# GLA chunks on one core: level products that move half the queries, seven level buffers, and the mixers' steps in other slots

## What is computed

```
def step(S, inp):
    qc, kc, vc, gc = inp
    Bc = jnp.cumsum(gc, axis=1)
    o_inter = jnp.einsum('blhd,bhdv->blhv', qc * jnp.exp(Bc), S)
    decay = jnp.exp(jnp.where(causal, Bc[:, :, None] - Bc[:, None, :], -jnp.inf))
    A = jnp.einsum('blhd,bshd,blshd->bhls', qc, kc, decay)
    o_intra = jnp.einsum('bhls,bshv->blhv', A, vc)
    BL = Bc[:, -1]
    S_new = jnp.exp(BL)[..., None] * S + jnp.einsum('bshd,bshv->bhdv', kc * jnp.exp(BL[:, None] - Bc), vc)
    return S_new, o_inter + o_intra
```

## Time and profile before

| | us |
|---|---|
| median of 3 runs | 2832.42 (2826.41 to 2833.7) |
| the profiled execution's own time | 2834.81 |
| its span | 2832.7 |
| PE busy | 2692.1 |
| DVE busy | 1515.3 |
| ACT busy | 1023.8 |
| mean granted clock of TensorE | 0.98 of full speed |

### The profile page before, as it was taken

One profiled execution on the slowest core, in us unless ns is written; L12 is line 12 of the kernel. 1 busy time (PEld: TensorE's weight loads), 2 busy tenths in 40 slices (PEclk: granted clock), 3 DMA queues, 4 the chain that ended last, 5 costly groups with the idle time before them and its releaser, 6 DMA issues.

```text
span 2832.7 us, 38394 instructions
## 1 busy us (share of the span) xinstructions
PE 2692.1 (95%) x16018; PEld 2416.0 (85%) x16018; DVE 1515.3 (53%) x2348; ACT 1023.8 (36%) x1453; POOL 0.2 (0%) x4
## 2 busy tenths in 40 slices
PE   5999999999999999988899999999899999999996
PEld 4889898877988998888889978997676978999996
DVE  4533464655366663466545675346764367544335
ACT  3444344432334333443333343344431334222222
POOL 0000000000000000000000000000000000000000
PEclk9999999999999999999999999999999999999998
DMA  4454435443325223532232333344224333322222
...
DMA packets 181727, 331.48 MB, mean 117 GB/s; under 512 B 19476, under 2 KB 98964, under 8 KB 181556
## 3 DMA queue, kind: packets, MB, share of 16 engines
...
...
## 4 chain that ended last, share of the span: by engine, by line
PE 84%; DVE 9%; ACT 3%; DMA 3%; issue 2%; SPq 0%; DVEq 0%; ACTq 0%
PE ps L775 74%; PE ps L926 2%; DMA w_stage<-w_down_in 1%; PE ps L995 1%; PE ps L989 1%; DVE n_xs L1386 1%; DVE Y L1383 1%; ACT w_hi L1022 1%; DVE w_lo L1307 1%; DMA w_stage<-w_in_in 1%; DVE n_normed L1402 1%; PE ps L853 1%; DVE Y L1351 1%; PE ps L882 1%; DVE HL L1398 1%
## 5 line engine op out<-in xcount | busy, mean ns | idle before, releaser
L775 PE MATMUL ps<-HH,w_lo 128*128 128x288 f32 (+1 forms) x3696 | 1024.4, 332 | 11.5 <-DVE HL L1398 6.7
L775 PE MATMUL ps<-HL,w_hi 128*128 128x288 f32 (+1 forms) x3696 | 1010.5, 328 | 0.0
L775 PE MATMUL ps<-HH,w_hi 128*128 128x288 f32 (+1 forms) x3696 | 1010.3, 328 | 0.0
L775 PEld LDWEIGHTS ps<-HH,w_lo 128*128 128x128 f32 x3696 | 631.4, 189 | 75.5 <-issue 18.8
L1307 DVE TENSOR_TENSOR w_lo<-w_stage,w_hi 128x1024 fp32r<-128x1024 f32 x396 | 483.9, 1222 | 364.2 <-ACT w_hi L1022 363.3
L775 PEld LDWEIGHTS ps<-HL,w_hi 128*128 128x128 f32 x3696 | 630.1, 189 | 49.4
L775 PEld LDWEIGHTS ps<-HH,w_hi 128*128 128x128 f32 x3696 | 630.4, 189 | 47.2
L1022 ACT ACTIVATE w_hi<-w_stage 128x1024 fp32r<-128x1024 f32 x396 | 416.2, 1053 | 412.4 <-PE ps L775 277.7
L775 PE MATMUL ps<-hid_hi,w_lo 128*128 128x288 f32 (+1 forms) x1056 | 302.4, 341 | 73.1 <-DVE Y L1351 54.9
L1351 DVE TENSOR_TENSOR Y<-ps,Y 128x512 f32<-128x512 f32 (+1 forms) x320 | 227.2, 722 | 159.2 <-PE ps L775 157.8
L775 PE MATMUL ps<-hid_lo,w_hi 128*128 128x288 f32 (+1 forms) x1056 | 294.9, 334 | 0.0
...
## 6 DMA issues: line engine op xcount, KB each, us to landing
...
```

The source lines that it names most:

```text
L775: mm = pe.matmul(ps[:, grp.bank + t, 0:W], wsl(w, k), x[:, k, t * W:(t + 1) * W], start=(q == 0 and m == 0), stop=(q == len(ks) - 1 and m ...
```

## The change

It has these parts.

1. A level's product moves only the queries of the second blocks: 64 columns instead of 128 (`q` in `level`), with the same 128 keys as weights. Four level results of 64 columns then share a PSUM bank in pairs (`LEVEL_BANK`), the masks have 64 columns for a level, and a merge writes only the second halves of A. The last level (w = 1) takes the keys as they are, so it has one argument and one factor instead of two.
2. There are seven level buffers. `vt` and `y_gated` share a place, as do `y_normed` and `k_decayed`; `vt` is loaded by a step of its own (`lvt`).
3. `lx` becomes `la1` (arguments of the decayed keys and of levels 0 to 2), `la2` (arguments of levels 3 to 6, `k_decayed`, `q_decayed`) and `la3` (factors of levels 0 to 3); `l1` makes the factors of levels 4 to 6 ahead of its merges. With u at G8, G10, G12, G14 (block 0's mixer) and G6 to G14 (block 1's), `la1` stands at the G unit u - 2, `la2` at the U unit u - 1, `la3` and `la` at the G unit u, `l1` and `l2` at the two D units, `lb` at U, `le` at G, and `lvt` at U.
4. W of the GLA layer comes five units later in block 0's case, behind U15 instead of G14, and two units later in block 1's, behind the second D instead of G16. The norm behind the first of them takes its eight `post` steps in pairs, and its `rstd` now hangs on a G unit with two D units behind it.
5. The mLSTM's steps of block 1 are put at other units: a chunk's `me` and the next one's `ma` stand together at a U unit each time. Those of block 0 stay where they were.

```
-        self.puts(B0[22:41])
+        self.puts(B0[22:46])
         self.wout(1, 0)
-        self.puts(B0[41:-2] + A1[:1] + B0[-2:] + A1[1:16])
+        self.puts(B0[46:-2] + A1[:1] + B0[-2:] + A1[1:16])
         self.proj(1, 1, 0, NPROJ)
-        self.puts(A1[16:47])
+        self.puts(A1[16:49])
         self.wout(1, 1)
-        self.puts(A1[47:-2] + B1[:1] + A1[-2:] + B1[1:])
+        self.puts(A1[49:-2] + B1[:1] + A1[-2:] + B1[1:])
...
-    u = mix(plan, 0, 0, at["P", 0, 0, 20, 0], 4)
+    u = mlstm(plan, 0, [(u, u + 1, u + 3, u + 4) for u in range(at["P", 0, 0, 22, 0], at["P", 0, 1, 13, 0], 4)])
...
-    u = mix(plan, 0, 1, at["G", 0, 0, 0, 0], 5)
+    u = at["G", 0, 0, 0, 0]
+    u = mlstm(plan, 1, [(u + 1, u + 3, u + 4, u + 7)] + [(v, v + 2, v + 5, v + 6) for v in range(u + 7, u + 25, 6)])
...
-    u = mix(plan, 1, 0, at["P", 1, 0, 18, 0], 6)
+    u = gla(plan, 0, at["P", 1, 0, 22, 0], [at["G", 0, 1, i, 0] for i in (8, 10, 12, 14)])
...
-    u = norm(2, 0, u + 1, ones, twos)
+    u = norm(2, 0, u + 1, twos, twos)
...
-    u = mix(plan, 1, 1, at["P", 1, 1, 18, 0], 6)
+    u = gla(plan, 1, at["P", 1, 1, 22, 0], [at["G", 1, 0, i, 0] for i in (6, 8, 10, 12, 14)])
...
+def gla(plan, blk, first, slots):
+    tag = plan.tag
+    tag(first, "lload", CHUNKS[blk][0])
+    for c, u in zip(CHUNKS[blk], slots):
+        tag(u - 2, "la1", c)
+        tag(u - 1, "la2", c)
+        tag(u, "la3", c)
+        tag(u, "la", c)
+        tag(u + 1, "l1" if c < NC else "l2", c)
+        if c < NC:
             tag(u + 2, "l2", c)
             tag(u + 3, "lb", c)
             tag(u + 4, "le", c)
-            if c != chunks[-1] or blk:
-                tag(u + 4, "lx", c + 1)
-            u += pace
-        u += 5 - pace
+            if c + 1 in CHUNKS[blk]:
+                tag(u + 5, "lvt", c + 1)
     if blk:
-        e, a = ("me", "ma") if layer == 0 else ("le", "la")
-        tag(u, a, NC)
-        u += 1
-        if layer:
-            tag(u, "l2", NC)
-            u += 1
-        for half in range(2):
-            for b in range(NB):
-                tag(u + b // 4, "ss", layer, NB * half + b)
-            u += 2
-            tag(u, "sh", layer, half)
-            u += 2
-        tag(u, e, NC)
-        u += 1
-    return u
+        return samples(plan, 1, u + 2, "le")
+    return u + 5
...
+def samples(plan, layer, u, last):
+    tag = plan.tag
+    for half in range(2):
+        for b in range(NB):
+            tag(u + b // 4, "ss", layer, NB * half + b)
+        tag(u + 2, "sh", layer, half)
+        u += 3
+    tag(u, last, NC)
+    return u + 1
...
+    LEVEL_BANK = ((3, 0), (3, 256), (2, 0), (2, 256), (0, 0), (0, 256), (1, 0), (3, 0))
+    def LEVEL(c, v):
+        return NLV * c + v if c < NC else NLV * NC + v - 4
...
-            def level(c, v, n):
-                x = g.x
-                b = (3, 2, 0, 1)[v % 4]
+            def level(c, v):
+                x, n = g.x, SIZE(c)
+                b, at = LEVEL_BANK[v]
                 if v < NLV:
-                    pe.wait_ge(s["level_ready"], (NLV * c if c < NC else NLV * NC - 4) + v + 1)
+                    pe.wait_ge(s["level_ready"], LEVEL(c, v) + 1)
                 for h in range(H):
+                    k = x.XL[:, v, h, 0:n] if v < NLV - 1 else x.QK[:, H + h, 0:n]
                     if v < NLV:
-                        lhs = rhs = x.XL[:, (NLV * c + v if c < NC else NLV * NC + v - 4) % 4, h, 0:n]
+                        w = LEVELS[v]
+                        m = n // 2
+                        q = x.XL[:, v, h, 0:n].rearrange("p (b u t) -> p b u t", u=2, t=w)[:, :, 1, :]
                     else:
-                        lhs, rhs = x.QK[:, H + h, 0:n], x.QK[:, h, 0:n]
-                    mm = pe.matmul(ps[0:n, M0 + b, h * L:h * L + n], lhs, rhs, start=True, stop=True)
+                        m, q = n, x.QK[:, h, 0:n]
+                    mm = pe.matmul(ps[0:n, M0 + b, at + h * m:at + (h + 1) * m], k, q, start=True, stop=True)
                 mm.then_inc(s["level_done"], 1)
             def l1(c):
-                for v in range(4):
-                    if v == 1:
-                        pe.wait_ge(s["k_copied"], NC + 1 + c + 1)
-                    if v == 2:
-                        pe.wait_ge(s["v_copied"], NC + 1 + c + 1)
-                    level(c, v, L)
+                level(c, 0)
+                level(c, 1)
+                pe.wait_ge(s["k_copied"], NC + 1 + c + 1)
+                level(c, 2)
+                level(c, 3)
             def l2(c):
-                if c == NC:
-                    pe.wait_ge(s["k_copied"], NC + 1 + c + 1)
-                    pe.wait_ge(s["v_copied"], NC + 1 + c + 1)
-                for v in range(4, 8):
-                    if c < NC:
-                        pe.wait_ge(s["merged"], 8 * c + v - 3)
-                    level(c, v, SIZE(c))
+                pe.wait_ge(s["v_copied"], NC + 1 + c + 1)
+                pe.wait_ge(s["k_copied"], NC + 1 + c + 1)
+                for v in range(4, NLV):
+                    level(c, v)
+                if c < NC:
+                    pe.wait_ge(s["merged"], 8 * c + 2)
+                level(c, NLV)
...
+                level_args(c, *((0, 3) if c < NC else (4, NLV)))
+            def la2(c):
+                x, n = g.x, SIZE(c)
+                q, k = x.QK[:, 0:H, 0:n], x.QK[:, H:2 * H, 0:n]
+                if c < NC:
+                    level_args(c, 3, NLV)
                 dve.wait_ge(s["qk_landed"], 16 * (NC + 1 + c + 1))
+                dve.wait_ge(s["kd_exp"], c + 1)
+                dve.tensor_tensor(x.KD[:, :, 0:n], x.KD[:, :, 0:n], k, ALU.mult).then_inc(s["kd_ready"], 1)
                 dve.wait_ge(s["eb"], c + 1)
                 dve.tensor_tensor(x.QW[:, :, 0:n], x.QW[:, :, 0:n], q, ALU.mult).then_inc(s["q_ready"], 1)
-                dve.wait_ge(s["kd_exp"], c + 1)
-                dve.tensor_tensor(x.KD[:, :, 0:n], x.KD[:, :, 0:n], k, ALU.mult).then_inc(s["kd_ready"], 1)
-                level_factors(c, v0, v1)
+            def la3(c):
+                level_factors(c, *((0, 4) if c < NC else (4, NLV)))
             def merge(c, v0, v1):
                 x, n = g.x, SIZE(c)
                 A = x.A[0:n, :, 0:n]
                 for v in range(v0, v1):
-                    i = 8 * c + (v if c < NC else v - 4)
-                    dve.wait_ge(s["level_done"], i + 1)
-                    if v == v0:
-                        wait(dve, s["num"], NC + c)
-                    wait(dve, s["merged"], i)
-                    dve.copy_predicated(A, g.lmask[0:n, v, 0:n].unsqueeze(1).to_broadcast([n, H, n]),
-                                        heads((3, 2, 0, 1)[v % 4], n)[0:n]).then_inc(s["merged"], 1)
+                    done = {0: 1, 2: 3, 4: 5}.get(v, v)
+                    i = 8 * c + (0 if c < NC else -4)
+                    dve.wait_ge(s["level_done"], i + done + 1)
+                    if c in (0, 4, NC) and v == v0:
+                        dve.wait_ge(s["cleared"], 1 + c // 4)
+                    wait(dve, s["num"], NC + c)
+                    wait(dve, s["merged"], i + v)
+                    b, at = LEVEL_BANK[v]
+                    if v < NLV:
+                        w, m = LEVELS[v], n // 2
+                        shape = [n, H, m // w, w]
+                        mask = g.lmask[0:n, v * L // 2:v * L // 2 + m].rearrange("p (b t) -> p b t", t=w)
+                        dve.copy_predicated(halves(A, w, 1), mask.unsqueeze(1).to_broadcast(shape),
+                                            ps[0:n, M0 + b, at:at + H * m].rearrange("p (h b t) -> p h b t", h=H, t=w)
+                                            ).then_inc(s["merged"], 1)
+                    else:
+                        mask = g.lmask[0:n, NLV * L // 2:NLV * L // 2 + n]
+                        dve.copy_predicated(A, mask.unsqueeze(1).to_broadcast([n, H, n]),
+                                            ps[0:n, M0 + b, 0:H * n].rearrange("p (h t) -> p h t", h=H)
+                                            ).then_inc(s["merged"], 1)
             def l1(c):
-                level_args(c, 4, 4)
+                level_factors(c, 4, NLV)
                 merge(c, 0, 4)
-                level_args(c, 4, NLV)
-                level_factors(c, 4, NLV)
             def l2(c):
-                if c == NC:
-                    dve.wait_ge(s["num"], 2 * NC)
-                    dve.memset(g.x.A[:, :, :], 0.0).then_inc(s["cleared"], 1)
-                    dve.wait_ge(s["cleared"], 3)
-                if c in (0, 4):
-                    dve.wait_ge(s["cleared"], 1 + c // 4)
-                merge(c, 4, 8)
+                merge(c, 4, NLV + 1)
```

149 lines of the change are left out of this document (75 added, 74 removed).

## The result

The changed kernel takes **2789.73 us** (median of 4 runs, 2785.85 to 2797.36), the kernel before 2832.91 beside it (4 runs, 2826.41 to 2833.7). The ratio is 0.9847, with a 95% interval of 0.9834 to 0.986: 43 us or 1.5% faster. The prediction said 2795 and gave 2768 to 2824. The profiled execution took 2786.02 us, 48.8 less than that of before; its span is 2784.2 us, its mean granted clock 0.987.

The account below looks back on a forecast made before the run. Bound: PE's waits for DVE's down-projection eviction around the mixers, plus slow clock behind them. Savings of 43.4, 12.0, 5.1 and 12.0 us, less new costs, took 2834.8 to 2797.5; median forecast 2795 us, range 2768 to 2824.

Parts of the forecast that it names:

- The level products: Level products of full chunks on PE: weight load of 128 keys sets the spacing, so moving 64 columns saves 0.
- Block 0's waits: D-unit waits in block 0's mixer: 3.6 us per chunk instead of 8.4, 14.4 over four chunks.
- (a): W of layer 1, block 0: U15 in between hides `y_lo`, removing a 3.7 us wait and 1.4 of clock, -5.1.
- (b): W in block 1, now directly behind the sample sequences' `le`: a new wait of about 2.3 us, +2.3.
- (c): Layer 1's sample steps now start at a D unit: shorter waits and no clock fall, -1.6 - 9.4 and -1.0.
- (d): Norm behind block 0's W: `rstd` on a G unit and paired `post` steps make DVE late at D units, +5.
- (e): mLSTM: `me` with `ma` at a U unit waits 1.2 us four times, once before; two 1.1 waits go, +1.4.
- Cheap products: Rival for level products: weight load hides behind the stream, 64 columns cost 0.067 us each; 2776 us, chance 0.12.
- the clock falls at half-wide products: Rival: PE streaming half the time for 3.5 us, twice a chunk, lowers its clock; 2822 us, chance 0.15.
- The waits only move: Rival: DVE meets each D unit among the chunks as late as before; 2842 us, chance 0.08.
- slower: Rival: the `k_decayed` wait keeps the clock low through chunk products, 9.4 us per chunk; 2870 us, chance 0.05.
- No new waits: Rival: ACT's exponentials don't delay `w_hi` and DVE keeps pace, so the chunks' 23.5 us go; 2771 us, chance 0.10.

Follow-up runs that it names:

- second trace: The changed kernel timed once more, unaltered, in a later set of runs beside the kernel before: 2793.69 us, ratio 0.986.
- the two experiments on widths: Half-wide level products and merges alone in the kernel before: ratio 1.001; the changed kernel with only 64 keys as level weights (incomplete output): ratio 0.9804.
- half-query experiment: The kernel before with only the half-wide level products and half-wide merges added: 2836.07 us against 2833.81, ratio 1.001.

## Why the prediction was right, point by point

**The ledger.** The prediction's terms add up to 17.5 us less idle time and 19.8 less busy time, 37.3 in all. Measured were 27.3 and, without the 9.3 us of the dense stretch, 11.9, which is 39.2 (24.4 and 15.3 in the second trace). The medians differ by 43 us, 40.6 in the second set. So the sum came close partly by luck: the idle time fell by 7 to 10 us more than summed, the chunks' new waits above all, the clock gave 4.5 to 8 less, and the two nearly cancel. By places, in us:

| term | predicted | measured |
|---|---|---|
| level products | 0 | 0 (53.0 against 52.6 busy) |
| the six long waits | -43.4 | -43.4, all gone |
| new waits, block 0's chunks | +14.4 | 1.5 + 2.28 + 2.23 + 2.21 = +8.2 |
| new waits, block 1's chunks | +9.1 | 2.43 + 2.37 + 2.37 = +7.2 |
| W of block 0, its wait | -3.7 | -3.7 |
| W of block 1 | +2.3 | +2.2 |
| sample steps and D unit, their waits | -2.6 | 0.65, less 2.63: -2.0 |
| the norm | +5 | 6.4, less the 2.6 it had: +3.8 |
| mLSTM | +1.4 | 7.8, less the 4.9 it had: +2.9 |
| D unit beside the later norm (2.87 for 4.30) | not named | -1.4 |
| idle elsewhere | 0 | -1.1 |
| clock behind six waits, W and samples; new falls | -22.8 + 3 | -11.9 |
| dense stretch of the last feed-forward | 0 | -9.3, not of the change |

**What bounds the kernel** was right: PE's waits at D units among the chunks and what the clock lost behind them. The places, the releaser and the double cost are all in the two traces.

**The level products** were right in size and reason. The small row with 4 columns moved and wide weights decided between the bounds, and the two experiments on widths show both sides: columns moved do nothing, weight columns do.

**Block 0's waits** had the right mechanism in each link, and were mis-sized: three waits of 1.2, 1.0 and 1.1 and a fourth of 0.3 were predicted, and 0.76, 0.72 and 0.80 came. The DVE timeline of the changed kernel, in the cycle whose t = 0 is at 1262.68:

```profile
1263.76 1.22 DVE L1575 TENSOR_TENSOR l_y_gated<-ps,l_y_gated 128x1024 f32<-128x1024 f32 x1 [2.23 <-PE ps L903]
...
1277.39 0.69 DVE L1657 TENSOR_TENSOR l_k_decayed<-l_k_decayed,l_qkb 128x512 f32<-128x512 f32 x1
...
1282.93 0.75 DVE L1373 TENSOR_TENSOR Y<-ps,Y 128x576 f32<-128x576 f32 x1
```

and ACT's:

```profile
1269.09 1.66 ACT L1248 ACTIVATE l_levels<-l_levels 128x512 f32<-128x512 f32 x3
1270.65 1.04 ACT L1045 ACTIVATE w_hi<-w_stage 128x1024 fp32r<-128x1024 f32 x1
```

`k_decayed` ends at t = 15.4, not 15.7; the first eviction begins at t = 20.25, not 20.8. The step that was mis-sized is "exponentials (0.66 each)". It took the spacing of a row of the kernel before. The last of that row's four stands by itself in a narrow window:

```profile
1303.20 0.63 ACT L1223 ACTIVATE l_levels<-l_levels 128x512 f32<-128x512 f32 x1
```

From 1301.19 to 1303.20 are three steps of 0.67 us. That is DVE's pace, not ACT's: each exponential needs a pair of arguments, and DVE makes one argument every 0.335 us. In the changed kernel ACT comes to the levels 0.4 us after their first pair is made and doesn't wait for the next ones: the three that start at 1269.09 hand over to `w_hi` at 1270.65, 0.52 each, which is its own pace. So `w_hi` begins at t = 8.0 rather than 8.3, and everything behind it is early. The other part is the fourth wait: the w_lo in front of the second eviction did not make PE wait, and in the first chunk `k_decayed` was in time as well, so that chunk has 1.5 where 3.6 stood. Block 1's 2.9 was too large in the same direction (2.4 measured).

**Block 1's first chunk**, predicted at 0.4, had no wait. **The clock**: +3 was taken for falls behind new waits, and that was too little. The busy time puts them at 22.8 - 11.9 = 10.9 us, 7.5 in the second trace. Windows of four microseconds show 6.6 of it: 0.58 and 0.60 behind two of block 1's waits, 0.67 and 0.50 behind the norm's 2.32 and 3.71. The prediction had one or two such falls, and there were four. The rest isn't placed.

**(a), (b) and (c)** stand as predicted: the 3.71 is gone, 2.22 came at 2183.58, and the first four sample steps of layer 1 go from 2111.56 to 2120.07, 8.5 us. (a) and (c) were also shown alone in the kernel before, 6 and 8 us by their ratios (intervals 2 to 10 and 5 to 11). **(d)** had the right place and a middle value between its bounds; the 2.6 us of waits that the norm already had there weren't subtracted. **(e)** was short by half: `me` with `ma` costs 1.20 three times and 1.36 once, nearly as said. The sample steps of layer 0 have four small waits (0.82, 0.45, 0.54, 0.65) where they had two (0.45, 1.08) besides the first one's, and one of 0.37 is new at 458; the prediction named none of these.

**DVE's busy time** fell by 16.3, not 25. As said, it had no meaning for the end: it fell by 11.5 in the half-query experiment (1515.3 to 1503.8), whose time didn't change.

**The rivals.** *Cheap products* and *the clock falls at half-wide products* are refuted: by the row of 3.68, and by a clock of 1.00 over block 0's mixer, half-wide products in it. *The waits only move* and *slower* are refuted by the 2.3 and 2.4 at each chunk; the transposes' wait did drop the clock, but for four microseconds, not for a chunk. *No new waits* is refuted as it stood, though 8 of the 23.5 us that it named did go.

What stays open: why a wait of 2.4 us lowers the clock in one execution and not in another at the same place; why the dense stretch took 9.3 us less in one execution at the same granted clock; how much the clock part is worth in the median, since only one execution of each set has a trace; and where a norm can stand among D units without these 6 us, which neither of the two experiments on it found.
